# Filling two waits of the matrix engine, and its idle start, with products that nobody reads, in a two-layer decoder step

## What is computed

```python
def moe_swiglu(h, router, w_gate, w_up, w_down):
    logits = jnp.einsum('btd,de->bte', h, router).astype(jnp.float32)
    top_v, top_i = lax.top_k(logits, TOP_K)
    gate = jax.nn.softmax(top_v, axis=-1)
    combine = jnp.einsum('btk,btke->bte', gate, jax.nn.one_hot(top_i, N_EXPERTS, dtype=jnp.float32))
    out = jnp.zeros(h.shape, jnp.float32)
    for e in range(N_EXPERTS):
        he = jax.nn.silu(h @ w_gate[e]) * (h @ w_up[e])
        out = out + combine[..., e:e + 1] * (he @ w_down[e])
```

## Time and profile before

| | |
|---|---|
| median of 3 runs | 1996.9 us (1996.71 to 1997.59) |
| the profiled execution, by the same clock | 1998.28 us |
| its span, first to last instruction | 1995.7 us |
| TensorE busy | 1961.5 us, 98% of the span |
| granted TensorE clock, mean over the span | 0.994 |
| start to the first product | 9.2 us |
| routing stretch, from the sums of squares to the first expert | 1083.9 to 1107.65 us |
| loop of the experts | 1107.65 to about 1976 us |

### The profile page before, as it was taken

How to read it: one execution, slowest core, us unless ns; L and a number is a source line. 1 busy time by engine, 2 the same in 40 slices (tenths; PEclk the granted TensorE clock), 3 DMA queues, 4 the chain that set the end, 5 groups by cost and what they waited for, 6 DMA issues and landing times.

```text
span 1995.7 us, 40349 instructions
## 1 busy us (share of the span) xinstructions
PE 1961.5 (98%) x17109; PEld 1400.9 (70%) x17109; DVE 474.0 (24%) x1223; ACT 298.4 (15%) x741; POOL 143.3 (7%) x246
## 2 busy tenths in 40 slices
PE   8999999999999999999999999999999999999996
PEld 6877777777777777777777476777777675647453
DVE  1353564220000134338433210101001001001011
ACT  2263231100000125422211100000000000000000
POOL 2221011000000000210000300000000000000000
PEclk9999999999999999999999999999999999999998
DMA  9645556464433344554532899999999999999996
GB/s 323 225 164 205 205 175 239 152 233 161 141 133 128 129 146 167 188 193 144 198 130 103 317 415 420 410 419 411 419 413 417 416 413 421 409 421 409 414 420 239
DMA packets 100121, 553.26 MB, mean 277 GB/s; under 512 B 13872, under 2 KB 30288, under 8 KB 41328
## 3 DMA queue, kind: packets, MB, share of 16 engines
q1 hardware_dynamic: 84432, 491.96, 62.9%
q0 software_dynamic: 12720, 48.97, 6.8%
q10 hardware_dynamic: 2800, 9.83, 1.4%
HBM read 532.08 MB, written 24.89 MB: 279 GB/s over the span
## 4 chain that ended last, share of the span: by engine, by line
PE 88%; issue 8%; DVE 2%; DMA 1%; POOL 0%; ACT 0%; POOLq 0%; DVEq 0%; SPq 0%
PE bank L490 38%; PE bank L1052 36%; PE bank L657 3%; PE bank L601 2%; PE bank L688 1%; PE bank L713 1%; PE bank L701 1%; DMA pages<-in_slc_pages 1%; PE bank L541 1%; PE bank L783 1%; PE bank L810 0%; DVE tmp L1916 0%; PE bank L851 0%; PE bank L919 0%; DMA wring<-in_wstream 0%
## 5 line engine op out<-in xcount | busy, mean ns | idle before, releaser
L1052 PE MATMUL bank<-wring,phase_region 128*32 128x512 f32 (+3 forms) x10112 | 868.4, 506 | 0.0
L1052 PEld LDWEIGHTS bank<-wring,phase_region 128*32 128x32 f32 x10112 | 561.7, 110 | 306.5 <-issue 148.2
L490 PE MATMUL bank<-xn,wring 128*128 128x288 f32 x2256 | 567.0, 409 | 9.8 <-DMA wring<-in_wstream 9.2
L490 PEld LDWEIGHTS bank<-xn,wring 128*128 128x128 f32 x2256 | 425.6, 191 | 134.1 <-DMA wring<-in_wstream 9.2
L490 PE MATMUL bank<-phase_region,wring 128*128 128x288 f32 x608 | 148.0, 406 | 0.6 <-DVE phase_region L2096 0.6
L2214 DVE TENSOR_TENSOR tmp<-phase_region,bank 128x512 f32<-128x512 f32 (+1 forms) x48 | 28.6, 595 | 500.9 <-PE bank L1052 500.9
L490 PEld LDWEIGHTS bank<-phase_region,wring 128*128 128x128 f32 x608 | 115.4, 190 | 32.9 <-DVE phase_region L2096 1.1
L1293 ACT ACTIVATE phase_region<-bank 128x512 f32<-128x512 f32 (+14 forms) x124 | 52.8, 464 | 425.2 <-PE bank L1052 296.5
L1584 ACT ACTIVATE phase_region<-bank 128x512 f32<-128x512 f32 (+1 forms) x48 | 26.1, 544 | 531.2 <-PE bank L1052 531.2
L2227 DVE COPY phase_region<-bank 32x256 f32<-32x256 f32 x32 | 13.5, 421 | 263.0 <-PE bank L1052 262.7
L657 PE MATMUL bank<-pages,wring 128*64 128x128 f32 (+1 forms) x1024 | 58.9, 276 | 0.0
(11 more groups left out here) (353 smaller groups left out, 1192.1 us busy)
## 6 DMA issues: line engine op xcount, KB each, us to landing
wring<-in_wstream SPq DMA_DIRECT2D x448, 1024.0 KB, 8.1
y_rows<-phase_region ACTq DMA_DIRECT2D x25, 384.0 KB, 7.5
pages<-in_cmp_pages POOLq DMA_DIRECT2D x64, 128.0 KB, 4.4
pages<-in_cmp_pages SPq DMA_DIRECT2D x64, 128.0 KB, 3.0
pages<-in_slc_pages SPq DMA_DIRECT2D x64, 128.0 KB, 4.4
pages<-in_slc_pages POOLq DMA_DIRECT2D x64, 128.0 KB, 4.8
out_win_keep<-in_win_rows POOLq DMA_DIRECT2D x2, 4064.0 KB, 26.6
pages<-in_win_kT POOLq DMA_DIRECT2D x4, 1024.0 KB, 5.3
```

The costliest lines, as they stand in the source:

```text
L490: mm = nc.tensor.matmul(ps[:, 0:width], wb, rhs(k), start=(k == 0), stop=(k == n - 1))
L1052: mm = nc.tensor.matmul(ps[QT * q:QT * q + QT, out0:out0 + n], lhsT, wring[:, a:a + n], start=start, stop=stop)
```

## The change

A new helper, `keep_busy(n)`, waits for the bank that the next group will take (without taking it) and issues n matmuls of `std` with itself, 128 weights columns and 288 moving columns, into that bank. The group that follows starts its sums anew, so nothing reads what was written. It is called three times: with 9 at the start, behind a new wait for `zeroed` and ahead of the first product; with 3 between `turn_tokens(0)` and the wait for `rT_ready`; with 3 between `turn_tokens(1)` and the wait for `cnt_ready`. At the start `std` is zero; in the routing stretch it holds what the layers left in it.

```diff
@@ -492,6 +492,14 @@
                         mm.then_inc(release, 1)
                 mm.then_inc(done, 1)
 
+            def keep_busy(n):
+
+                u = uses[0]
+                if u >= 8:
+                    pe.wait_ge(bank_free[u % 8], u // 8)
+                for _ in range(n):
+                    nc.tensor.matmul(psum[u % 8][:, 0:T], std[:, 0:P], std[:, 0:T], start=True, stop=True)
+
             def strip_sums(key, n, lhs, rhs):
 
                 ps, done = bank(key)
@@ -547,6 +555,8 @@
                 mm.then_inc(done, 1)
 
             ident = C("ident")
+            pe.wait_ge(S["zeroed"], 1)
+            keep_busy(9)
             for l in range(DEPTH):
 
                 product(("in", l, 0), KD, lambda k: weighted_tile(l, 0, k))
@@ -975,6 +985,7 @@
             mm.then_inc(done, 1)
             rms_spread(DEPTH - 1, 1)
             turn_tokens(0)
+            keep_busy(3)
             pe.wait_ge(S["rT_ready"], 1)
             ps, done = bank(("router",))
             for tt, (t0, n) in enumerate(TILES):
```

## The result

The change takes 2002.36 us, the median of 20 runs, against 1997.45 us for 20 runs of the kernel before beside it. The ratio is 1.0025, with a 95% interval of 1.0019 to 1.0031: it is slower by some 4.9 us, where 1991.0 us was forecast. The profiled execution of the change took 2006.33 us, a high one among the 20, with a span of 2004.6 us and a mean granted clock of 0.994.

A forecast was written before the change was run, and what follows sets the result against it. TensorE, busy for 98% of the span, was taken as the bound, gaining only where it idles or works slowly. From the median of 1996.9 us, 3.0 (start) and 2.9 (routing stretch) were subtracted: 1991.0 us, range 1989.0 to 1996.5.

The forecast's parts named there:

- The start, 3.0 us: First product: nine hidden filling matmuls raise the clock, so it takes 3.9 us and not 6.94; bounds -1.0 and +3.0.
- 12.9: Start: matmul rows taken to run at half clock, about 6.2 us, before the clock rises.
- Can the rest follow 3.0 us sooner? ... The gain passes to the end: After the first product: weights land in time for the next products, so the start's 3.0 us reaches the end.
- The routing stretch, 2.9 us: Routing waits: fillings hold full clock, gather starts at 1097.5, experts at 1104.7 instead of 1107.65; at most 5.1 us.
- the rival in which the clock falls onto the gather: Routing stretch: clock falls after the counting products, experts start 3.0 to 4.6 us late; about 1997.5 us, chance 0.13.
- The rule of the Trainium skill that transposes don't count for the clock: Routing stretch: contradicted by the trace, which the sum followed; by the rule the time would be near 1997.
- The table of passes ... moves to 1103.7 and stays ahead: Before the experts' loop: the table, done at 1105.22 before, comes at 1103.7, ahead of the experts' start at 1104.7.
- fillings hidden: Start and both routing waits: fillings end before what TensorE waits for, with 0.2 and 0.3 us to spare in routing.
- The rival of fillings that don't count: Start and routing: fillings run at half clock and delay work by 1.0 and 2.3 us; 2000.2 us, chance 0.09.

The follow-up runs named there:

- e6: Kernel before plus only the nine products at the start, with GpSimd's first part of the exchange copies issued ahead of its page loads: 1995.47 us, 0.9994.
- e7: The change with six instead of nine products at the start, and GpSimd's first exchange copies ahead of its page loads: 1998.40 us, ratio 1.0002 against before.
- e4: The change with six instead of nine products at the start and 52 very small ones behind them (256 instructions): 1997.13 us, ratio 0.9999 against before.
- e2: Kernel before plus only the two fillings of three products in the routing stretch, none at the start: 1995.11 us, ratio 0.9986.
- e5: e4 with GpSimd's first part of the exchange copies issued ahead of its page loads: 1995.05 us, ratio 0.9990 against the kernel before.
- e9: The change plus 49 small products at the start (256 instructions) and GpSimd's first exchange copies ahead of its page loads: 1994.10 us, 0.9984 against before.
- e11: The change with two instead of three products per routing wait (52 instructions) and GpSimd's first exchange copies ahead of page loads: 2000.92 us, 1.0018 against before.
- e10: The change once more, unaltered, for a second profile: 2005.04 us in its one execution.
- e3: Kernel before plus 15 very small products of zeros ahead of the first product (60 instructions), no filling: 2002.65 us, ratio 1.0030.

## Why the prediction was wrong

Its two gains are there, and the end does not have them.

- **The start, 3.0 us**: right in its mechanism and size; 2.77 measured, hidden as predicted. The rise came after ten rows, not 12.9.
- **"Can the rest follow 3.0 us sooner? ... The gain passes to the end"**: the first step that failed. It looked at the weights alone. VectorE's reciprocal had 1.0 us to spare and hangs on a copy that does not move with TensorE; 0.56 us passed. The table of waits that I read shows what was late, not what was nearly late, and the timeline of before had the answer: the reciprocal ends at 61.31, its reader starts at 62.33. e6 shows that with this chain moved, 2.5 to 2.7 us do pass.
- **The routing stretch, 2.9 us**: in the profile of the change the clock stayed at 1.00, and the gather came 2.92 us sooner, as forecast. That it stayed up was luck: of the other seven profiles with fillings in these waits only e7's shows the same; in e4 it fell behind the counting products, and in e2, e5, e9, e11 and the change's second profile (e10) just ahead of the gather, which then took 6.22 to 6.67 us. So the rival in which the clock falls onto the gather was real in a mild form, 3.4 us at half clock. It cost the loop next to nothing: from the sums of squares to the first expert it is 22.25 us in e2 and 22.26 in e10, against 22.12 in the change without the fall, because the loop starts 2.0 us behind the start of the count's read in all three (1103.66 to 1105.70 in e2), and the read waits for VectorE's table. The rule of the Trainium skill that transposes don't count for the clock was not put to a further test, since fillings now stand between the transposes.
- **"The table of passes ... moves to 1103.7 and stays ahead"**: the second step that failed. It compared the table with the experts' start and left out the 2.0 us between them, for the read of the count and the loop's set-up. So 1.64 us passed, and 1.51 in e2.
- **What was not there at all**: the sum had no term for 60 instructions being there. They cost 5.0 us, some 440 us behind the last of them, at a branch that the change does not touch; e3 shows it with no filling at all. This is the step that turned a gain into a loss: "fillings hidden" was argued for their time, and nothing for their place; no rival ended slower by that way. The rival of fillings that don't count had a time near the one measured (2000.2) by a mechanism that did not occur.

By the steps that repeat, - 0.56 - 1.64 + 5.0 is + 2.8 us. The median is + 4.9. The other 2 us are of the size of a fall of the clock (1.7), and both profiles of the change have falls at places where the profile of before has none. The runs without a profile bear it out: the mean granted clock is 0.9937 in the first profile, where 3.4 us were lost near 340 us and 1.7 at the turn, and 0.9941 over the change's runs. That is 0.8 us less lost, so an estimate from these figures is 2.6 us a run outside the turn, a part of it at the gather, where it costs next to nothing. Why the clock falls in one execution and not in the next is not shown. The idle of 1.34 us near 340 us has no cause that I could show, and e7's time outside its span has none either. Which instruction has to lie where in its block for the turn to stall was not found: between 48 and 52 it begins, and where it ends, between 60 and 256, was not tried.

## What to carry to other kernels

Instructions that do nothing for the result still take place in the code: where a long program has a loop, compare the duration of the loop's branch before and after any change in the number of instructions ahead of it, and try a few paddings before judging the change. When a stage is to come sooner, list for each later join what ends within the gain of being late, since a table of waits names only what is late already; here one chain with 1.0 us to spare took 2.2 of 2.8 us. And count what lies between a table and the loop that reads it.

## What the runs showed of the hardware

- A branch back to the head of a loop of some 10,000 instructions took 0.42 to 0.44 us or 4.8 to 6.0 us, by the place of the code modulo 256 instructions. A packet of q8 moved 2.3 to 3.8 us behind its start in either case; the quick branch was over by then, the slow one was not. The idle that followed, 3.2 to 4.35 us, had half clock for about 3.4 us behind it in all four kernels that stalled.
- Products of zeros lifted the clock: in the change ten matmul rows of them started 0.48 us apart, the next eight 0.2437.
- After a wait of 1.9 us between filling and work the clock fell 1.1 us into the work (e7); after 0.81 us it did not (the change).
- A fall of the clock came in one execution and not in another of the same code (behind the wait at 60 us: 5.34 us for the product in e10, 3.65 in the change).
- The read of one number into a register and the set-up of a loop cost TensorE 2.0 us from the number's last write to the loop's first product (the change, 1109.06 to 1111.03).
